# Other byte offsets for the stationary tiles of a two-layer decoder trunk on one core

## The reference, cut to what matters

```
def swiglu(h, w_gate, w_up, w_down):
    return (jax.nn.silu(h @ w_gate) * (h @ w_up)) @ w_down

for layer in range(DEPTH):                     # DEPTH = 2
    x = x + 0.5 * swiglu(rmsnorm(x, ...), ffn_w_gate[layer, 0], ffn_w_up[layer, 0], ffn_w_down[layer, 0])
    h = rmsnorm(x, norm_gain[layer, 1])
    x = x + mixer(h, ...)                      # conv_sparse_attn_mixer or gated_deltanet_mixer
    x = x + 0.5 * swiglu(rmsnorm(x, ...), ffn_w_gate[layer, 1], ffn_w_up[layer, 1], ffn_w_down[layer, 1])
return rmsnorm(x, final_gain)
```

## The kernel before, in words

| stationary, by moving | matmuls | columns | offset |
|---|---|---|---|
| p by h, emix, omix | about 2700 | 512 | 0 |
| ab, a22, s12, s43 by h and t | 5880 | 256 | 64 |
| d0 by a | 32 units | 512 | 128 |
| d2 by a | 31 units, and 66 matmuls of 256 | 512 | 192 |
| emix by ik_dup, k_dup | 112 | 128 to 512 | 0 |

## Time and profile before

### The profile page before, as it was taken

The page is one execution under the profiler, slowest core; times in us unless marked ns, Lnnn a source line. Parts: engine busy times, 40 slices in busy tenths (PEclk is TensorE's granted clock), DMA queues, the critical chain, the costliest instruction groups (busy, mean ns, idle before and its releaser), DMA issues.

```text
span 1996.9 us, 30677 instructions
## 1 busy us (share of the span) xinstructions
PE 1967.4 (99%) x12159; PEld 1733.6 (87%) x12159; DVE 1386.3 (69%) x1928; ACT 978.3 (49%) x1472; POOL 516.9 (26%) x530
## 2 busy tenths in 40 slices
PE   9999999999999999999999999999999999999998
PEld 7898998787788988998898999878888888989996
DVE  6964977588647955973894696376766558946963
ACT  5543653445645633653562464355564555524642
POOL 1201311454221301311130221157566111302311
PEclk9999999999999999999999999999999999999999
DMA  5232332444122232332233223222222122332331
GB/s 189 94 129 85 106 130 72 121 130 135 54 85 95 106 118 83 110 126 82 95 114 104 90 107 125 72 77 96 69 77 92 53 95 95 114 108 85 117 127 43
DMA packets 63167, 199.95 MB, mean 100 GB/s; under 512 B 12816, under 2 KB 14896, under 8 KB 63024
## 3 DMA queue, kind: packets, MB, share of 16 engines
q1 hardware_dynamic: 59616, 196.55, 29.2%
q10 hardware_dynamic: 3408, 1.44, 0.3%
HBM read 188.51 MB, written 2.38 MB: 96 GB/s over the span
## 4 chain that ended last, share of the span: by engine, by line
PE 87%; DVE 6%; ACT 3%; issue 2%; POOL 1%; DMA 1%; ACTq 0%; SPq 0%; DVEq 0%; POOLq 0%
PE prod L590 16%; PE prod L592 15%; PE prod L591 15%; PE misc L684 6%; PE misc L685 6%; PE misc L686 6%; PE prod L684 4%; PE prod L685 4%; PE prod L686 4%; PE misc L905 2%; DVE h_lo L1619 1%; ACT L1443 0%; ACT h_hi L1156 0%; PE misc L784 0%; PE prod L980 0%
## 5 line engine op out<-in xcount | busy, mean ns | idle before, releaser
L590 PE MATMUL prod<-h_hi,p_hi 128*128 128x512 f32 x728 | 300.6, 413 | 2.2 <-DVE p_lo L1503 1.3
L592 PE MATMUL prod<-h_hi,p_lo 128*128 128x512 f32 x728 | 285.3, 392 | 0.0
L591 PE MATMUL prod<-h_lo,p_hi 128*128 128x512 f32 x728 | 284.4, 391 | 0.0
L590 PE MATMUL prod<-a_hi,d_hi 128*128 128x512 f32 x693 | 273.3, 394 | 0.0
L591 PE MATMUL prod<-a_lo,d_hi 128*128 128x512 f32 x693 | 272.8, 394 | 0.0
L592 PE MATMUL prod<-a_hi,d_lo 128*128 128x512 f32 x693 | 272.6, 393 | 0.0
L1503 DVE TENSOR_TENSOR d_lo<-raw,d_hi 128x1408 fp32r<-128x1408 f32 x64 | 104.0, 1626 | 240.1 <-ACT d_hi L1070 240.0
L2100 POOL TENSOR_TENSOR s_f<-raw 128x512 f32<-128x512 f32 x70 | 94.4, 1348 | 675.0 <-DVE s_lo L1578 361.9
L1070 ACT ACTIVATE d_hi<-raw 128x1408 fp32r<-128x1408 f32 x64 | 88.4, 1381 | 227.1 <-PE prod L592 226.5
L1503 DVE TENSOR_TENSOR p_lo<-raw,p_hi 128x1024 fp32r<-128x1024 f32 x86 | 111.6, 1298 | 77.4 <-ACT p_hi L1070 77.1
L590 PEld LDWEIGHTS prod<-h_hi,p_hi 128*128 128x128 f32 x728 | 137.2, 188 | 31.0 <-issue 8.5
(11 more groups left out here) (371 smaller groups left out, 5267.7 us busy)
## 6 DMA issues: line engine op xcount, KB each, us to landing
raw<-in_w SPq DMA_DIRECT2D x252, 512.0 KB, 3.4
raw<-in_wd SPq DMA_DIRECT2D x64, 704.0 KB, 4.2
blk<-blocks SPq DMA_DIRECT2D x16, 256.0 KB
x<-in_x SPq DMA_DIRECT2D x8, 256.0 KB, 5.9
k_dup<-k_dup SPq DMA_DIRECT2D x8, 256.0 KB, 3.5
silu_g<-g_rows SPq DMA_DIRECT2D x7, 256.0 KB, 4.8
out<-y_out SPq DMA_DIRECT2D x12, 128.0 KB, 1.9
raw<-in_w SPq DMA_DIRECT2D x4, 256.0 KB, 6.0
```

Of the source, the lines that this page charges most:

```text
L590: pe.matmul(bank, wh, hi, start=k == 0, stop=False)
L591: pe.matmul(bank, wh, lo, start=False, stop=False)
L592: ins = pe.matmul(bank, wl, hi, start=False, stop=k == tiles_n - 1)
```

## The change

It gives the stationary tiles other byte offsets and drops the names `p_hi`, `p_lo`: plain units now use the tiles `ab0` and `s43`, which lie at offset 0 for this. `ab1`, `a22` and `s12` stay at 64. All wide tiles `d` come to offset 0. The tile `t3` (high, low and float) is shifted by 48 elements, 192 bytes, so `s43` by `t3` has offset 64 as before; the rooms for `t_hi` and `t_lo` grow by 256 bytes each.

```
+W_STEP = 64
+T_STEP = (0, 0, 0, 48)
+T_ROOM = (4 * KT // 2 * TOKENS + 64) * 4
...
-        plain_w = [tuple(w_part(f"p_{part}{i}", at + 2 * QB * j, 2 * QUAD) for j, part in enumerate(("hi", "lo")))
-                 for i, at in enumerate((0, 14 * QB + ALIGN))]
-        wide = [tuple(w_part(f"d_{part}{i}", at + HALF * P * 4 * j, HALF * P) for j, part in enumerate(("hi", "lo")))
-                for i, at in enumerate((2 * W_SHIFT, 4 * QB + 2 * W_SHIFT, 14 * QB + 3 * W_SHIFT))]
-        ab_hi_w = [w_part(f"ab_hi{i}", W_SHIFT + 6 * QB * i, 2 * QUAD) for i in range(2)]
-        s43_hi_w, s43_lo_w = w_part("s43_hi", W_SHIFT + 14 * QB, 2 * QUAD), w_part("s43_lo", W_SHIFT + 16 * QB, 2 * QUAD)
+        ab_at, s43_at = (0, 6 * QB + W_STEP), 14 * QB + 4 * W_STEP
+        a22_at, s12_at = 4 * QB + W_STEP, 10 * QB + W_STEP
+        ab_hi_w = [w_part(f"ab_hi{i}", ab_at[i], 2 * QUAD) for i in range(2)]
+        s43_hi_w, s43_lo_w = w_part("s43_hi", s43_at, 2 * QUAD), w_part("s43_lo", s43_at + 2 * QB, 2 * QUAD)
+        wide = [(w_part(f"d_hi{i}", at, HALF * P), w_part(f"d_lo{i}", at + HALF * P * 4, HALF * P))
+                for i, at in enumerate((0, 4 * QB + 4 * W_STEP, s43_at))]
...
-            return plain_w[0]
+                return s43_hi_w, s43_lo_w
+            return ab_hi_w[0], ab_lo_w[0]
...
         t_hi, t_lo, t_f = ([nc.alloc_sbuf_tensor_at(f"{n}{i}", [P, KT // 2, TOKENS], dt, offset=t_at + part * T_ROOM
-                                                    + i * KT // 2 * TOKENS * 4) for i in range(4)]
+                                                    + (i * KT // 2 * TOKENS + sum(T_STEP[:i + 1])) * 4) for i in range(4)]
```

More of the change, by code:

```diff
@@ L198 @@
 TOKENS = T // 2
-W_SHIFT = 64
-T_ROOM = 4 * KT // 2 * TOKENS * 4
+W_STEP = 64
+T_STEP = (0, 0, 0, 48)
+T_ROOM = (4 * KT // 2 * TOKENS + 64) * 4
 WARM = 5
@@ L251, in program @@
         QB = QUAD * 4
-        w_all = sb("w_all", [(18 * QB + 2 * (HALF - KT) * P * 4 + ALIGN) // 4])
+        w_all = sb("w_all", [(18 * QB + 2 * (HALF - KT) * P * 4 + 4 * W_STEP) // 4])
         def w_part(name, at, cols):
             return nc.alloc_sbuf_tensor_at(name, [P, cols], F32R, offset=w_at + at)
-        plain_w = [tuple(w_part(f"p_{part}{i}", at + 2 * QB * j, 2 * QUAD) for j, part in enumerate(("hi", "lo")))
-                 for i, at in enumerate((0, 14 * QB + ALIGN))]
-        wide = [tuple(w_part(f"d_{part}{i}", at + HALF * P * 4 * j, HALF * P) for j, part in enumerate(("hi", "lo")))
-                for i, at in enumerate((2 * W_SHIFT, 4 * QB + 2 * W_SHIFT, 14 * QB + 3 * W_SHIFT))]
-        ab_hi_w = [w_part(f"ab_hi{i}", W_SHIFT + 6 * QB * i, 2 * QUAD) for i in range(2)]
-        ab_lo_w = [w_part(f"ab_lo{i}", W_SHIFT + 6 * QB * i + 2 * QB, 2 * QUAD) for i in range(2)]
-        a22_hi_w, a22_lo_w = w_part("a22_hi", W_SHIFT + 4 * QB, QUAD), w_part("a22_lo", W_SHIFT + 5 * QB, QUAD)
-        s12_hi_w, s12_lo_w = w_part("s12_hi", W_SHIFT + 10 * QB, 2 * QUAD), w_part("s12_lo", W_SHIFT + 12 * QB, 2 * QUAD)
-        s43_hi_w, s43_lo_w = w_part("s43_hi", W_SHIFT + 14 * QB, 2 * QUAD), w_part("s43_lo", W_SHIFT + 16 * QB, 2 * QUAD)
+        ab_at, s43_at = (0, 6 * QB + W_STEP), 14 * QB + 4 * W_STEP
+        a22_at, s12_at = 4 * QB + W_STEP, 10 * QB + W_STEP
+        ab_hi_w = [w_part(f"ab_hi{i}", ab_at[i], 2 * QUAD) for i in range(2)]
+        ab_lo_w = [w_part(f"ab_lo{i}", ab_at[i] + 2 * QB, 2 * QUAD) for i in range(2)]
+        a22_hi_w, a22_lo_w = w_part("a22_hi", a22_at, QUAD), w_part("a22_lo", a22_at + QB, QUAD)
+        s12_hi_w, s12_lo_w = w_part("s12_hi", s12_at, 2 * QUAD), w_part("s12_lo", s12_at + 2 * QB, 2 * QUAD)
+        s43_hi_w, s43_lo_w = w_part("s43_hi", s43_at, 2 * QUAD), w_part("s43_lo", s43_at + 2 * QB, 2 * QUAD)
+        wide = [(w_part(f"d_hi{i}", at, HALF * P), w_part(f"d_lo{i}", at + HALF * P * 4, HALF * P))
+                for i, at in enumerate((0, 4 * QB + 4 * W_STEP, s43_at))]
         def weights(n):
@@ L273, in weights @@
             if (u + (f or 0)) % 2:
-                return plain_w[1]
-            return plain_w[0]
+                return s43_hi_w, s43_lo_w
+            return ab_hi_w[0], ab_lo_w[0]
         consts = sb("consts", [len(CONSTS), P])
@@ L319, in program @@
         snap_a = ffn("snap_a", [2, TOKENS])
-        snap_d = nc.alloc_sbuf_tensor_at("snap_d", [P, 2, TOKENS], F32, offset=w_at + 18 * QB + ALIGN)
+        snap_d = nc.alloc_sbuf_tensor_at("snap_d", [P, 2, TOKENS], F32, offset=w_at + s43_at + 4 * QB)
         sq0 = nc.alloc_sbuf_tensor_at("sq0", [P, KT, T], F32, offset=t_at)
```

## The result

The changed kernel takes 2012.86 us (median of 5 runs, 2012.32 to 2013.24), the kernel before 1998.84 us: a ratio of 1.0072, with a 95% interval of 1.0057 to 1.0086. It is slower by 14 us. The forecast was 2000.3 us with a range of 1989 to 2003.5 us, so the time lies outside the range, and "no change" was wrong too.

What follows compares the result with a forecast made beforehand. PE's own pace was taken as the bound; -9.4 + 10.5 + 0.2 + 0.2 = +1.5 us on a span of 1996.9 us, with 1.9 us around it, gave 2000.3 us. The range, for 8 times in 10, was 1989 to 2003.5 us.

Steps and rivals of the forecast that it cites:

- Bound (PE's own pace is the time): Whole kernel: PE, busy 99% of the span, sets the time as cost per matmul times their number.
- Down units, -9.4 us: Down units, offsets 128 and 192 to 0: 2079 matmuls of 512 columns save 4.6 ns each, less 0.2 us.
- s43 and ab0 by h at offset 0, +10.5 us: Fast pairs, 64 to 0: 1483 matmuls of 256 columns at 120 instead of 113.3 ns, plus 0.6 us for leaving runs.
- The last unit, +0.2 us: Last unit, offset 192 to 0: 66 matmuls of 256 columns at 120 instead of 117.6 ns.
- When a run is left, the first matmul after it is charged: Fast pairs: after each of 101 runs at offset 0, one matmul costs 6 ns more, 0.6 us in all.
- the hand-over from t3 to ab1: Fast pairs: ab1 loaded under t3's end has offset 128, one matmul in some 31 pairs, 6 ns each, +0.2 us.
- s12, a22 and s43 by t stay at 276: Fast pairs: the groups of these products, still at offset 64, were to keep their mean duration of 276 ns.
- ab by h about 279: Fast pairs: the group of ab by h, mixing both buffers, was to read about 279 ns.
- Nothing holds these units: Down units: nothing but PE holds them, as weights are made as fast as PE frees buffers; no wait added or removed.
- rival 1: Fast pairs: offset 0 becomes free for 256 columns after settling; 1990.4 us, halfway case about 1995; chance 0.30 including halfway.
- rival 2: Down units: they don't come into step at offset 0, so their gain is 0; 2009.7 us; chance 0.08.
- rival 3: Whole change: it does nothing because the offset isn't the cause; 1998.8 us; chance 0.05.

Runs made afterwards that it cites:

- the down-only one: The kernel before with only the wide tiles d moved to offset 0, fast tiles left at 64 and plain tiles at 0: 2005.86 us.

## Why the prediction was wrong

- *Bound (PE's own pace is the time).* Right. There is no new wait, and the difference of the spans is accounted for by distances between matmuls.
- *Down units, -9.4 us.* Right: -9.7 us by the starts, distances of 226.7 ns, groups at 389 ns.
- *s43 and ab0 by h at offset 0, +10.5 us.* The price of 120.0 ns was right and steady; with ab0's first half at 118.2 ns it comes to 8.7 us in the steady pairs, and the pairs with waits add 0.7 us at most. The reason given for it is not shown. It took PEld's shares of 100% and 81% for the room that a load has, but PEld's records are 188 ns in both stages, longer than the 113.3 ns from one start to the next, so they don't tell how long a load takes.
- *The last unit, +0.2 us.* As forecast: +0.1 us, 283 ns.
- *"When a run is left, the first matmul after it is charged", 0.6 us; the hand-over from t3 to ab1, "one matmul in each of some 31 pairs", 0.2 us; "s12, a22 and s43 by t stay at 276".* This is the step that failed: a hand-over was priced as one matmul, and it sets the pace of all that follow. I had one row of fast pairs at 113.3 ns and took it for the price of the shape at this offset. It is one of two steady paces. A pair with ab0 was to last 0.23 us longer and one with ab1 0.08; they last 0.40 and 0.36 us longer. The products at offset 64 rose to 117.8 ns, 13.6 us, because the down units now hand over in the rhythm of offset 0, because in the pairs with ab0 its run at offset 0 leaves the stream in the slow pace, and because in the others the hand-over from the shifted t3 to ab1 does. With these 13.6 us and t3's 1.3 us in place of the 0.6 and 0.2 us, my sum would have been 2014.4 us; 2012.86 was measured. "ab by h about 279" came near the measured 280 by luck: ab1 was to stay at 276 there and didn't.
- *"Nothing holds these units", no cover, no wait.* Right, and beside the point: I looked for coupling between stages in engines and buffers, and it lies in the stream of PE itself.
- *The rivals.* Offset 0 does not become free (rival 1: 120.0 ns in runs of 24 and more). The down units do come into step (rival 2). The change does do what it says (rival 3). None of them holds the 4 ns of the untouched products, and neither did the range.

A hint was in the rows before: behind the last down matmul the first distance is 0.12 us and the next 0.113, so the stream comes into its pace from somewhere. A stronger one was in the same trace, in the first down block. These are the starts of its second, third, fourth and fifth unit:

```profile
133.84 0.39 PE L590 MATMUL prod<-a_hi,d_hi 128*128 128x512 f32 x1
...
141.40 0.40 PE L590 MATMUL prod<-a_hi,d_hi 128*128 128x512 f32 x1
...
149.07 0.40 PE L590 MATMUL prod<-a_hi,d_hi 128*128 128x512 f32 x1
...
156.77 0.39 PE L590 MATMUL prod<-a_hi,d_hi 128*128 128x512 f32 x1
```

The second and the fourth unit both use d2, at offset 192, for 33 matmuls of the same shape: 7.56 us and 7.70 us, 229.1 and 233.3 ns each. One offset had two steady paces before anything was changed, and the means over d0 and d2 hide it.

The prediction drew from the Trainium skill, "TensorE: Matmul & The Clock Gate", section "Step-by-step: what each phase is for", that no offset costs anything, since a weight load doesn't take read bandwidth from the running matmul. The runs don't agree with that for these shapes: with nothing but its weights' offset changed, from 0 to 64, the last down unit of a block takes 233.4 ns for each 512-column matmul instead of 226.7 (the kernel with the last unit at 64 against the down-only one). What the two reads share is not shown.

## What to carry to other kernels

When PE is busy 99% of the span and its distances repeat to a nanosecond or two, the price of a matmul may depend on what ran before it. Before a row is used as a price per shape, look whether the same shape has another steady distance elsewhere in the trace, and compare counts per 90 us window before and after in the stages that the change doesn't touch. A gain in one stage is only sure once the stage behind it shows its old pace; here changing one unit in eight at the hand-over made the difference between +7 us and -9 us.

## What the runs showed of the hardware

- The distance between matmuls depends on the address of the next stationary tile minus that of the stream, modulo 256 bytes. With 512 columns: 226.7 ns at 0, 229.0 or 233.3 at 192, mostly 232.6 at 128, 233.3 at 64. With 256 columns: 120.0 at 0, 118.3 at 32, 113.3 or 117.8 at 64, 117.3 (in one stage 118.7) at 96, 117.6 at 192.
- At 64 the two paces with 256 columns both lasted through stages of eleven pairs, 105 and 109 us. One hand-over with another offset moves the stream between them, and behind a wait of PE it takes one or the other.
- Open: what in the memory or the engine makes these paces (no run looks below the distances), and whether the last distance is the cause of the pace behind it or goes with it.
